# Expert rows of tiles 1 and 2 gathered as joined 8 KB rows, slot by slot, in a fused layer kernel

## The chip, the cores and the metric

One core of one Trainium2 chip runs the whole kernel. The metric is the device time of one execution in microseconds (us). Its median over 3 runs was 1422.61 us (1419.26 to 1423.8).

## What is computed

One layer of a diffusion transformer on 384 tokens (128 context tokens, 256 latent tokens), width 1024, all in f32: modulation, differential attention and a gated DeltaNet side by side, an output projection, and then PEER expert retrieval, which is where the change lies. Cut to that:

```python
def peer(h, w_pq, sub_keys, expert_u, expert_v):     # 8 heads, 2 x 128 keys, top 16
    q = (hf @ w_pq).reshape(T, PEER_HEADS, 2, PEER_DK // 2)
    s = jnp.einsum('thpd,hpnd->thpn', q, sub_keys)
    sv, si = lax.top_k(s, PEER_TOPK)
    cand = ...                                       # 16 x 16 sums per head
    top_s, pos = lax.top_k(cand, PEER_TOPK)
    eidx = ...                                       # 128 experts of 16384 for each token
    gates = jax.nn.softmax(top_s, axis=-1)
    a_sel = hf . expert_u[eidx]
    coef = gates * jax.nn.gelu(a_sel)
    return sum over the 128 experts of coef * expert_v[eidx]
```

Each token takes 128 experts, each a row of 1024 f32 (4 KB) in expert_u and one in expert_v. That is 384 x 128 x 2 rows of 4 KB, 403 MB of gathered data.

## The kernel before, in words

Tokens lie in three tiles (NT = 3) of 128, one token in each partition. A tile has SLOTS = 128 expert slots, and two halves a of HALF = 64 slots. The choice of experts (choice_steps, L473) runs by quarters of 32 slots on VectorE (DVE): `top_key`, `pair_sums`, `top_pair`, `places`, `chosen` twice and `experts`, which writes the indices of the quarter; its scores come from `query` and `key_score` on TensorE (PE).

A **U gather** (`u_rows`, L967, the DMA at L977) is one indirect DMA on GpSimd (POOL): for slot n it brings to each partition its token's row of expert_u, 128 rows, 512 KB. VectorE's `dot` (L2086) multiplies it by the token's h (hnow, in PSUM) and sums it into coef[:, n]. When the 64 dots of a half are done, `coef` (ACT L1305, DVE L2101, PE) applies Gelu, multiplies by the gates and transposes, and `fill` (ACT L1318, L1324) spreads coefficients into W. A **V gather** (`v_rows`, L981, the DMA at L988) brings rows of expert_v by `rowT`, the transposed indices: one gather carries the 64 experts of each of two tokens, and a `v_batch` (PE, L1357) takes four such gathers and multiplies them by 128 x 32 blocks of W into acc, 8 matmuls with 512 columns in four column strips. After the last batch of a tile, `take` (L2112, L2118) multiplies by the gate and adds to xs, `last_norm` (L2124 to L2128) normalizes, and SP stores y (L885). So the gathers run in an order of halves: 64 U, 64 V, 64 U, 64 V of tile 0, then of tile 1, then of tile 2, 768 in all (`gather_order`, HALVES, ALONE).

Rows land in slots of 4 KB per partition. STAGES lists which are usable at which place in the order; from place 208 on there are 13: twelve in the buffer big and one in hT. `row_homes` gives each gather the slot that was used longest ago, and `row_free` (L948) makes POOL wait until the user of that slot's last row has finished (`dot_ready` for U rows, `vsum_done` for V rows).

The order of instructions on PE, DVE, ACT and POOL is made when the kernel is built: each step has costs by engine and a list of the steps it follows (`layer_steps`, `expert_steps`). `Plan.ranked` sorts the steps by the longest chain to the end, plus the head start of the table EARLIER, and `place` puts each in the first gap of its engines that holds it. Each engine runs its list strictly in that order. DVE takes 5.7 for a `top_key`, 1.16 for a `dot`; PE takes 3.6 for half a `query` in this plan.

The weight chunks of `query` of tiles 1 and 2 are shared. Chunk (pq, 2, 1) is loaded by SP (L853) when `query` (0, 2) of tile 2 is done, so the second half of tile 1's choice comes after that, and so does tile 2's.

Of the kernel before, what the change touches and what calls it, by code (L numbers as in the profile page):

```python
# [11 lines left out]
P = 128  # L12
D = 1024
KD = D // P
NT = 3
# [62 lines left out]
HALVES = [(t, a) for t in range(NT) for a in range(2)]  # L78
ALONE = {(0, 0): 64, (0, 1): 64, (1, 0): 64, (1, 1): 64, (2, 0): 64}
# [3 lines left out]
def gather_order():  # L83


    out = [("gu", 0, n) for n in range(HALF)]
    for k, (t, a) in enumerate(HALVES):
        mine = [("gv", t, a, b, j) for b in range(BATCHES) for j in range(QUADS)]
        following = [("gu", u, HALF * c + n) for u, c in HALVES[k + 1:k + 2] for n in range(HALF)]
        first = ALONE.get((t, a), 0)  # L90
        out += mine[:first]
        for n in range(0, len(mine) - first, QUADS):
            out += mine[first + n:first + n + QUADS] + following[n:n + QUADS]
        rest = len(mine) - first
        out += following[rest:]
    return out
# [6 lines left out]
def row_homes():  # L103


    out, uses, last = {}, [0] * (ROWS + 13), [-1] * (ROWS + 13)
    for n, g in enumerate(GATHERS):
        slot = min([homes for until, homes in STAGES if n < until][0], key=lambda s: last[s])
        uses[slot] += 1
        out[g] = (slot, 16 * uses[slot], GATHERS[last[slot]] if last[slot] >= 0 else None)  # L110
        last[slot] = n
    return out
# [11 lines left out]
OPS_ROWS = [g for g in GATHERS if HOMES[g][0] > ROWS + 8]  # L124


def row_user(gather):

    return ("dot",) + gather[1:] if gather[0] == "gu" else ("v_batch",) + gather[1:4]
# [30 lines left out]
EARLIER = {('experts', 0, 0, 0): 200.0, ('slot_gates', 1, 0): 15.0, ('experts', 1, 0, 0): 50.0, ('experts', 1, 0, 1): 50.0, ('dn_done', 1, 1): 50.0, ('v_batch', 0, 0, 15): 100.0, ('dn_done', 2, 1): 100.0, ('dn_done', 1, 0): 100.0, ('dot', 0, 63): 100.0, ('slot_gates', 2, 0): 100.0, ('coef', 1, 0): 200.0, ('qk_turn', 2): 150.0, ('dn_scores', 1, 0): 200.0, ('value', 2, 3): 100.0, ('dn_p', 1, 1, 3): 75.0, ('o_turn', 2): 100.0, ('da_turn', 2): 15.0, ('query', 3, 1): 200.0, ('expert_rows', 0, 0): 150.0, ('dn_scores', 2, 0): 200.0, ('top_key', 0, 0): 50.0, ('mod', 5): 30.0, ('value', 1, 3): 30.0, ('qk_turn', 1): 100.0, ('coef', 0, 1): 100.0, ('experts', 2, 0, 1): 50.0, ('top_key', 2, 0): 100.0, ('token', 1, 2): 200.0, ('resid', 0, 1): 15.0, ('mod', 9): 15.0, ('experts', 0, 0, 1): 15.0, ('experts', 0, 1, 0): 30.0, ('experts', 2, 1, 1): 100.0, ('dn_vb', 2, 0): 15.0, ('dn_vb', 1, 1): 100.0, ('h_turn', 2): 100.0, ('dn_vb', 2, 1): 75.0, ('dn_done', 2, 0): 50.0, ('expert_rows', 0, 1): 15.0}  # L160
# [312 lines left out]
def choice_steps(add, t):  # L473
# [16 lines left out]
    for hh in range(2):  # L490
        for q in range(2):
# [5 lines left out]
            add(("experts", t, hh, q), ("DVE", 0.5), after=[("chosen", t, hh, q, 1), ("expert_rows", t, 0) if hh else None]  # L497
# [3 lines left out]
        add(("expert_rows", t, hh), ("PE", 0, 0.2, ("expert_rows", t, hh), 1), ("DVE", 0.5),  # L501
            after=[("experts", t, hh, 0), ("experts", t, hh, 1), ("dot", 0, SLOTS - 1) if t == 2 else None])


def expert_steps(add):

    for n, g in enumerate(GATHERS):
        t = g[1]
        after = [("@", 1, GATHERS[n - 1])] if n else [(k,) + td for td in PAIRS[0] for k in ("dn_scores", "dn_qg")]
        after += [("experts", t, g[2] // HALF, g[2] // QUARTER % 2)] if g[0] == "gu" else [("expert_rows", t, g[2])]  # L510
        slot, _, back = HOMES[g]
        if back:
            after.append(row_user(back))
# [6 lines left out]
        add(g, ("POOL", 1.12), ("DMA", 0, 1.12, None), ("LATE", 0, 1.2, None), after=after)  # L520
    for k, (t, a) in enumerate(HALVES):
        before = HALVES[k - 1] if k else None
        if t and not a:
            add(("h_load", t), ("ACT", 1.4), after=[("dot", t - 1, SLOTS - 1), ("h_turn", t)])
        for n in range(HALF * a, HALF * a + HALF):
            add(("dot", t, n), ("DVE", 1.16), after=[("gu", t, n), ("dot", t, n - 1) if n else ("h_load", t) if t else ("h_turn", 0)])
        add(("coef", t, a), [("ACT", 0, 3.5), ("DVE", 2.1, 0.4), ("PE", 2.6, 0.15, ("coef", t, a), 1)],
            after=[("dot", t, HALF * a + HALF - 1), ("slot_gates", t, a), ("mod_turn", 11)] + [("dn_decay",) + td for td in PAIRS[2]] + [("fill",) + HALVES[k - 2] + (FILLS - 1,) if k > 1 else None])
        for b in range(BATCHES):
            if b % 4 == 0:  # L530
# [5 lines left out]
                after=[("gv", t, a, b, QUADS - 1), ("fill", t, a, b // 4), ("take", t - 1) if t and not a and not b else None,  # L536
                       ("v_batch", t, a, b - 1) if b else ("v_batch",) + before + (BATCHES - 1,) if k else None])
        if a:
            add(("take", t), ("DVE", 3.0), after=[("v_batch", t, 1, BATCHES - 1), ("gate", 1, min(t, 1), 1),
# [22 lines left out]
def program(nc, counts, x, cst, msk, par, wch, wba, kcT, vc, s0, subk, eu, ev, nout,  # L562
# [4 lines left out]
    with ctx:  # L567
# [134 lines left out]
        def row(slot):  # L702

            if slot == ROWS + 8:
                return hT[:, 0].rearrange("p k n -> p (k n)")
            if slot > ROWS + 8:
# [1533 lines left out]
```

## Time and profile before

| | before |
|---|---|
| median of 3 runs | 1422.61 us (1419.26 to 1423.8) |
| span of the profiled execution | 1577.7 us (its own unprofiled time isn't given) |
| PE, DVE, ACT, POOL busy | 865.6, 813.6, 277.6, 749.9 us |
| DMA, mean over the span | 486.09 MB, 308 GB/s |
| issue of the first and last gather | 276.6 us, 1559.0 us |

The profiled execution is 155 us longer than the median of the runs. In the windows below the columns are the stretch in us from the span's start, its length, the busy time of PE, PEld (weight load), DVE, ACT and POOL with their instruction counts, the mean granted TensorE clock (1.00 is 2.4 GHz, 0.50 is 1.2 GHz), the busy share of the 16 DMA engines, and GB/s. In a timeline a row is: start us, length us, engine, line, operation, out<-in, count, and in brackets the idle time before it and what ended it.

### The profile page before, as it was taken

Reading aid. Unit: us, or ns where it says so; the run is one execution under the profiler, and the core shown is the slowest. Engines: PE = TensorE matmul, PEld = TensorE weight load, DVE = VectorE, ACT = ScalarE, POOL = GpSimd, SP = SyncE. Lnnn points to the kernel's source line nnn. Section 1 sums busy time; section 2 is a strip of 40 time slices with the busy share of each in tenths; the row PEclk is TensorE's granted clock in tenths of the full one; section 3 lists DMA queues with packets and bytes.
Section 4 is the critical chain, followed back from the end, with each engine's and each line's share of the span. In section 5 each row is a group of like instructions: output and inputs, shape, how many; then the busy total and the mean of one; then the engine's idle time right before and its main releaser. Section 6 shows DMA issues by size and latency. Waiting matters only on the chain.

```text
span 1577.7 us, 14365 instructions
## 1 busy us (share of the span) xinstructions
PE 865.6 (55%) x4990; PEld 500.8 (32%) x4990; DVE 813.6 (52%) x2047; ACT 277.6 (18%) x662; POOL 749.9 (48%) x794
## 2 busy tenths in 40 slices
PE   4999998799567776787620675400442005500254
PEld 2566867556353355543210651000110001100010
DVE  2443234687484277851597146897515760087301
ACT  4234443122241232421000020000100000000000
POOL 0001000453446644456676226676667666676663
PEclk9998999899798999899755887655685557755576
DMA  9234446995659988799999729999999999999996
GB/s 394 91 140 151 161 167 254 375 390 215 240 182 356 343 310 316 241 395 352 364 404 357 297 72 375 359 397 364 354 376 376 402 346 335 359 402 364 347 368 234
DMA packets 120295, 486.09 MB, mean 308 GB/s; under 512 B 13344, under 2 KB 14240, under 8 KB 115616
## 3 DMA queue, kind: packets, MB, share of 16 engines
q0 software_dynamic: 111056, 404.28, 68.4%
q1 hardware_dynamic: 9168, 80.90, 13.2%
q8 instruction: 41, 0.67, 0.2%
q14 instruction: 30, 0.25, 0.0%
HBM read 482.50 MB, written 2.62 MB: 307 GB/s over the span
## 4 chain that ended last, share of the span: by engine, by line
DVE 17%; issue 17%; PE 14%; POOL 13%; DMA 6%; another core or an unknown queue 4%; ACT 1%; POOLq 0%; DVEq 0%; ACTq 0%
PE bank L1357 13%; DVE big L2086 11%; POOL big L988 10%; DMA big<-in_ev,idx 2%; POOL big L977 2%; DMA big<-in_ev,rowT 2%; DMA big<-in_eu,consts 2%; DVE hT L2086 1%; POOL hT L988 1%; PE bank L1363 1%; PE bank L1475 0%; DVE big L1876 0%; DVE dn_tok L1970 0%; DVE sq L2112 0%
## 5 line engine op out<-in xcount | busy, mean ns | idle before, releaser
L2086 DVE CUSTOM_DVE_ANT_0 big<-big,hnow 128x1024 f32<-128x1024 f32 x315 | 377.4, 1218 | 193.2 <-DMA big<-in_eu,consts 127.9
L1357 PE MATMUL bank<-big,W 128*32 128x512 f32 x1296 | 259.7, 835 | 167.6 <-DMA big<-in_ev,idx 64.0
L977 POOL DMA_INDIRECT big<-in_eu,consts x236 | 223.4, 947 | 103.4 <-issue 71.6
L988 POOL DMA_INDIRECT big<-in_ev,rowT x197 | 190.5, 967 | 153.5 <-PE bank L1357 76.6
L1357 PE MATMUL bank<-hT,wring 128*128 128x128 f32 (+1 forms) x896 | 143.3, 319 | 40.4 <-issue 32.2
L1363 PE MATMUL bank<-consts 128*128 128x128 f32 x6 | 2.4, 392 | 294.3 <-DVE consts L2101 294.3
L1357 PEld LDWEIGHTS bank<-big,W 128*32 128x32 f32 x1296 | 53.4, 136 | 332.3 <-issue 319.7
L988 POOL DMA_INDIRECT big<-in_ev,idx x118 | 111.7, 947 | 68.2 <-issue 33.3
L1357 PEld LDWEIGHTS bank<-hT,wring 128*128 128x128 f32 x896 | 120.4, 202 | 64.6 <-issue 41.4
L1357 PE MATMUL bank<-big 128*128 128x128 f32 x720 | 100.1, 288 | 40.6 <-issue 23.0
L977 POOL DMA_INDIRECT big<-in_eu,idx x79 | 75.1, 951 | 99.1 <-DVE coef L2086 57.4
L1357 PEld LDWEIGHTS bank<-big 128*128 128x128 f32 x720 | 91.1, 200 | 48.8 <-issue 28.7
L1363 PEld LDWEIGHTS bank<-consts 128*128 128x128 f32 x6 | 1.0, 161 | 298.4 <-DVE consts L2101 298.2
L1357 PE MATMUL bank<-hT,W 128*32 128x512 f32 x120 | 83.9, 839 | 10.3 <-DMA big<-in_ev,rowT 5.9
L1357 PE MATMUL bank<-wring,hT 128*128 128x512 f32 x176 | 78.8, 606 | 6.1 <-DMA wring<-in_wch 6.1
L1003 ACT ACTIVATE big<-bank 128x512 f32<-128x512 f32 x84 | 49.6, 597 | 110.8 <-PE bank L1357 84.9
L1876 DVE TENSOR_TENSOR big<-bank,masks 128x512 f32<-128x512 f32 x42 | 28.8, 688 | 73.9 <-PE bank L1475 54.6
L900 POOL DMA_DIRECT2D out_o_ck<-tok x1 | 0.7, 732 | 138.4 <-ACT tok L1003 138.4
L1357 PE MATMUL bank<-wring,W 128*32 128x512 f32 x300 | 50.9, 670 | 12.5 <-DMA wring<-in_wch 6.5
L988 POOL DMA_INDIRECT wring<-in_ev,rowT x39 | 37.0, 949 | 40.1 <-DVE coef L2086 14.5
L1305 ACT ACTIVATE coef<-coef 128x64 f32<-128x64 f32 x4 | 1.0, 256 | 285.6 <-remote 139.7
L2112 DVE TENSOR_TENSOR sq<-bank,gate 128x512 f32<-128x512 f32 x6 | 4.1, 688 | 88.8 <-PE bank L1357 88.0
(294 smaller groups left out, 1379.8 us busy)
## 6 DMA issues: line engine op xcount, KB each, us to landing
wring<-in_wch SPq DMA_DIRECT2D x29, 2048.0 KB, 9.2
big<-in_wch SPq DMA_DIRECT2D x6, 1536.0 KB, 8.8
big<-in_eu,consts POOLq DMA_INDIRECT x236
big<-in_ev,rowT POOLq DMA_INDIRECT x197
tok<-in_wch SPq DMA_DIRECT2D x6, 512.0 KB, 9.9
big<-in_ev,idx POOLq DMA_INDIRECT x118
xs<-in_x SPq DMA_DIRECT2D x1, 1536.0 KB, 6.6
out_y<-xs SPq DMA_DIRECT2D x3, 512.0 KB
```

Source lines behind the costliest of these rows:

```text
L900: pool.dma_start(o_ck, tok[:, 0, 512:1024]).then_inc(cache_out, 16)
L977: nc.gpsimd.indirect_dma_start(row(slot), None, eu, bass.IndirectOffsetOnAxis(ap=idx[t][:, n:n + 1], axis=0)).then_inc(rows_in[slot], 16)
L988: nc.gpsimd.indirect_dma_start(row(slot), None, ev, bass.IndirectOffsetOnAxis(ap=rowT[t][:, n:n + 1], axis=0)).then_inc(rows_in[slot], 16)
L1003: nc.scalar.activation(out, ps(*job)[:, 0:n] if src is None else src, func, **kw).then_inc(*reads(sig, key, *job))
L1305: nc.scalar.activation(c, c, ACT.Gelu).then_inc(*gelu_ready.next(t, a))
L1357: return nc.tensor.matmul(out, lhsT, rhs, start=first, stop=last)
L1363: ins = nc.tensor.transpose(b[:, i * P:(i + 1) * P], src[:, i * P:(i + 1) * P], ident)
L1876: V.tensor_tensor(heads(PM[pi][d]), heads(ps(*job)[:, :]), rep(level_mask(d, lv), 4), ALU.mult).then_inc(*reads(p_ready, (t, d, lv), *job))
L2086: V.tensor_tensor_reduce(row(slot), row(slot), hnow[:, :], 1.0, 0.0, ALU.mult, ALU.add, coef[t % 2][:, n:n + 1]).then_inc(dot_ready, 1)
L2112: ins = V.tensor_tensor(sq[:, :], acc[h][:, :], gate[:, v, s], ALU.mult)
```

## The change

Tile 0 stays as it is: U and V gathers of 4 KB rows, 64 by 64, in the same slots. For tiles 1 and 2 a new input `euv` holds each expert's U row and V row side by side (8 KB). One gather per slot (`wide_rows`, 128 rows, 1 MB) brings both by the slot's own index. So 512 gathers of 512 KB become 256 of 1 MB. `dot` reads the first 4 KB. After each pair of dots, ACT applies Gelu to the pair's two coefficients, DVE's new `spread` writes for each slot a 128 x 128 diagonal matrix (identity times coefficient times gate), and PE's new `v_slot` multiplies it by the last 4 KB of the row into acc, two matmuls with 512 columns for each slot. The transposes, the coef step, the fills and `rowT` go for tiles 1 and 2. Wide slots are pairs of the 4 KB slots: six in big for tile 1 (each waits for the last users of both rows under it), ten for tile 2 (four more in wring, after the last `query`). Eight diagonal matrices fit in W (SPREADS), and `v_slot` (1, 0) waits for tile 0's `take`.

```diff
-HALVES = [(t, a) for t in range(NT) for a in range(2)]
-ALONE = {(0, 0): 64, (0, 1): 64, (1, 0): 64, (1, 1): 64, (2, 0): 64}
+HALVES = [(0, 0), (0, 1)]
+WIDE0 = ROWS + 13
+WIDE = {1: range(WIDE0, WIDE0 + 6), 2: range(WIDE0, WIDE0 + 10)}
+SPREADS = 8
...
+    for a in range(2):
+        out += [("gu", 0, HALF * a + n) for n in range(HALF)]
+        out += [("gv", 0, a, b, j) for b in range(BATCHES) for j in range(QUADS)]
+    return out + [("gw", t, n) for t in (1, 2) for n in range(SLOTS)]
...
-EARLIER = {... ('experts', 2, 1, 1): 100.0, ...}
+EARLIER = {... ('experts', 2, 1, 1): 400.0, ... ('experts', 2, 1, 0): 400.0, ('last_norm', 0): 300.0, ('last_norm', 1): 150.0}
...
+        add(g, ("POOL", 1.12), ("DMA", 0, 2.5 if g[0] == "gw" else 1.12, None), ("LATE", 0, 1.2, None), after=after)
...
+            add(("gelu", t, b), ("ACT", 0.3), after=[("dot", t, 2 * b + 1)])
+            add(("spread", t, b), ("DVE", 0.45),
+                after=[("gelu", t, b), ("slot_gates", t, 2 * b // HALF),
+                       ("v_slot", 1 + old // SLOTS, old % SLOTS) if old >= 0 else ("v_batch", 0, 1, BATCHES - 1)])
+            for n in (2 * b, 2 * b + 1):
+                add(("v_slot", t, n), ("PE", 1.75),
+                    after=[("spread", t, b), ("v_slot", t, n - 1) if n else ("take", t - 1)])
...
+            def wide_rows(t, n):
+                if n % QUARTER == 0:
+                    pool.wait_ge(*idx_ready.at(t, n // QUARTER))
+                slot, _ = row_slot(("gw", t, n))
+                row_free(("gw", t, n))
+                nc.gpsimd.indirect_dma_start(row(slot), None, euv,
+                                             bass.IndirectOffsetOnAxis(ap=idx[t][:, n:n + 1], axis=0)
+                                             ).then_inc(rows_in[slot], 16)
...
+            def gelu(t, b):
+                c = coef[t % 2][:, 2 * b:2 * b + 2]
+                act.wait_ge(dot_ready, SLOTS * t + 2 * b + 2)
+                nc.scalar.activation(c, c, ACT.Gelu).then_inc(*gelu_ready.next(t, b))
...
+            def v_slot(t, n):
+                if n == 0:
+                    pe.wait_ge(*acc_read.at(t - 1))
+                slot, count = row_slot(("gw", t, n))
+                pe.wait_ge(rows_in[slot], count)
+                pe.wait_ge(*spread_ready.at(t, n // 2))
+                for h in range(2):
+                    ins = mm(acc[h][:, :], spread_at(t, n), row(slot)[:, D + 512 * h:D + 512 * h + 512], n == 0, n == SLOTS - 1)
+                ins.then_inc(vsum_done, 1)
...
+            def spread(t, b):
+                old = SLOTS * (t - 1) + 2 * b + 1 - SPREADS
+                dve.wait_ge(vsum_done, 2 * BATCHES + max(old + 1, 0))
+                dve.wait_ge(*gelu_ready.at(t, b))
+                for n in (2 * b, 2 * b + 1):
+                    ins = V.scalar_tensor_tensor(out=spread_at(t, n), in0=ident, scalar=coef[t % 2][:, n:n + 1],
+                                                 in1=gates[t][:, n:n + 1].to_broadcast([P, P]), op0=ALU.mult, op1=ALU.mult)
+                ins.then_inc(*spread_ready.next(t, b))
...
+        "euv": np.concatenate([a["expert_u"][0], a["expert_v"][0]], 1), "nout": rows(a["norm_out"]),
```

## Rows read from the trace of the kernel before

**Rows 1.** The page: span, busy times, and the slices of 39.4 us.

```profile
span 1577.7 us, 14365 instructions
...
PE 865.6 (55%) x4990; PEld 500.8 (32%) x4990; DVE 813.6 (52%) x2047; ACT 277.6 (18%) x662; POOL 749.9 (48%) x794
...
PEclk9998999899798999899755887655685557755576
DMA  9234446995659988799999729999999999999996
```

**Rows 2.** Windows: all of tiles 1 and 2, then single stretches.

```profile
774.00:1560.00 786.00, 252.47 (x1479) 96.17 (x1479) 410.59 (x975) 36.03 (x92) 487.34 (x512) 0.63 0.92 351
...
881.00:935.00 54.00, 46.16 (x385) 42.45 (x387) 5.67 (x23) 11.21 (x22) 0.51 (x1) 0.94 0.32 128
935.00:1008.00 73.00, 39.16 (x213) 8.19 (x205) 52.40 (x268) 3.58 (x11) 50.22 (x51) 0.73 0.95 349
...
1096.00:1189.00 93.00, 41.73 (x226) 9.14 (x226) 36.64 (x136) 9.09 (x23) 61.25 (x65) 0.68 0.97 364
1189.00:1277.00 88.00, 5.49 (x32) 1.18 (x32) 67.55 (x111) 0.00 (x0) 60.39 (x65) 0.54 0.98 381
...
1410.00:1440.00 30.00, 0.00 (x0) 0.00 (x0) 24.84 (x41) 0.00 (x0) 22.27 (x24) 0.50 1.03 409
```

**Rows 3.** The page's DMA queues: packets, MB, share of 16 engines.

```profile
q0 software_dynamic: 111056, 404.28, 68.4%
q1 hardware_dynamic: 9168, 80.90, 13.2%
```

**Rows 4.** The chain of waits from 774 us: start, length, what.

```profile
811.20 2.42 issue
...
828.00 51.60 issue
```

**Rows 5.** The page's costliest groups: dots and U gathers of tiles 1, 2.

```profile
L2086 DVE CUSTOM_DVE_ANT_0 big<-big,hnow 128x1024 f32<-128x1024 f32 x315 | 377.4, 1218 | 193.2 <-DMA big<-in_eu,consts 127.9
...
L977 POOL DMA_INDIRECT big<-in_eu,consts x236 | 223.4, 947 | 103.4 <-issue 71.6
```

**Rows 6.** Timeline: one v_batch at either clock, with the last gather.

```profile
1155.75 1.92 PE L1357 MATMUL bank<-big,W 128*32 128x512 f32 x16 [2.06 <-DMA big<-in_ev,rowT]
...
1559.04 0.95 POOL L988 DMA_INDIRECT big<-in_ev,idx  x1 [0.30 <-issue]
1564.94 3.64 PE L1357 MATMUL bank<-big,W 128*32 128x512 f32 x16 [6.99 <-DMA big<-in_ev,idx]
```

**Rows 7.** Timeline: Gelu's table load, the half's product, two small DVE operations.

```profile
927.47 1.28 ACT L1305 ACT_TABLE_LOAD   x1
928.76 0.26 ACT L1305 ACTIVATE consts<-consts 128x64 f32<-128x64 f32 x1
929.12 0.29 DVE L2101 TENSOR_TENSOR consts<-consts,params 128x128 f32<-128x128 f32 x1 [54.41 <-ACT consts L1305]
...
714.10 0.23 DVE L2052 SCALAR_TENSOR_TENSOR E<-E 128x64 f32<-128x64 f32 x1
```

**Rows 8.** Timeline: a gather after a pause of POOL, and its dot.

```profile
1198.66 0.95 POOL L977 DMA_INDIRECT big<-in_eu,consts  x1 [3.21 <-remote]
...
1203.01 1.22 DVE L2086 CUSTOM_DVE_ANT_0 big<-big,hnow 128x1024 f32<-128x1024 f32 x1 [0.79 <-DMA big<-in_eu,consts]
```

**Rows 9.** Windows, DVE alone: the choice of one quarter, twice.

```profile
932.10:947.10 15.00, 14.21 (x73) 0.73 0.62 199
...
748.40:766.00 17.60, 14.16 (x72) 0.82 0.98 361
```

**Rows 10.** Timeline of SP and PE: a weight chunk's load and a query.

```profile
889.24 0.33 SPq L853 DMA_DIRECT2D wring<-in_wch  x1
...
899.45 7.31 PE L1357 MATMUL bank<-hT,wring 128*128 128x128 f32 x64
```

**Rows 11.** Window with PE busy 72% of the time.

```profile
550.00:600.00 50.00, 35.85 (x247) 28.82 (x236) 36.21 (x76) 18.75 (x51) 20.77 (x22) 0.93 0.88 315
```

More of the change, by code:

```diff
@@ L103, in row_homes @@
 def row_homes():
-    out, uses, last = {}, [0] * (ROWS + 13), [-1] * (ROWS + 13)
+    out, uses, last = {}, [0] * (WIDE0 + 10), [-1] * (WIDE0 + 10)
     for n, g in enumerate(GATHERS):
-        slot = min([homes for until, homes in STAGES if n < until][0], key=lambda s: last[s])
+        homes = WIDE[g[1]] if g[0] == "gw" else [homes for until, homes in STAGES if n < until][0]
+        slot = min(homes, key=lambda s: last[s])
         uses[slot] += 1
-        out[g] = (slot, 16 * uses[slot], GATHERS[last[slot]] if last[slot] >= 0 else None)
+        under = [slot]
+        if last[slot] < 0 and WIDE0 <= slot < WIDE0 + 6:
+            under = [2 * (slot - WIDE0), 2 * (slot - WIDE0) + 1]
+        out[g] = (slot, 16 * uses[slot], [GATHERS[last[u]] for u in under if last[u] >= 0])
         last[slot] = n
@@ L121, in row_slot @@
     return HOMES[gather][:2]
-OPS_ROWS = [g for g in GATHERS if HOMES[g][0] > ROWS + 8]
+OPS_ROWS = [g for g in GATHERS if HOMES[g][0] in range(ROWS + 9, WIDE0)]
 def row_user(gather):
-    return ("dot",) + gather[1:] if gather[0] == "gu" else ("v_batch",) + gather[1:4]
+    return {"gu": ("dot",) + gather[1:], "gv": ("v_batch",) + gather[1:4], "gw": ("v_slot",) + gather[1:]}[gather[0]]
 class Counts:
@@ L496, in choice_steps @@
                 add(("chosen", t, hh, q, w), ("DVE", 2.0), after=[("places", t, hh, q), ("chosen", t, hh, q, 0) if w else None])
-            add(("experts", t, hh, q), ("DVE", 0.5), after=[("chosen", t, hh, q, 1), ("expert_rows", t, 0) if hh else None]
+            add(("experts", t, hh, q), ("DVE", 0.5), after=[("chosen", t, hh, q, 1), ("expert_rows", 0, 0) if hh and not t else None]
                 + [("dn_decay", u, d) for u in (1, 2) for d in range(2) if t])
@@ L519, in expert_steps @@
             after.append(("dn_done",) + PAIRS[2][slot // 4])
-        add(g, ("POOL", 1.12), ("DMA", 0, 1.12, None), ("LATE", 0, 1.2, None), after=after)
-    for k, (t, a) in enumerate(HALVES):
[L522 to L526, printed above, removed]
+        add(g, ("POOL", 1.12), ("DMA", 0, 2.5 if g[0] == "gw" else 1.12, None), ("LATE", 0, 1.2, None), after=after)
+    for t in range(NT):
+        if t:
+            add(("h_load", t), ("ACT", 1.4), after=[("dot", t - 1, SLOTS - 1), ("h_turn", t)])
+        for n in range(SLOTS):
+            add(("dot", t, n), ("DVE", 1.16), after=[("gw" if t else "gu", t, n), ("dot", t, n - 1) if n else ("h_load", t) if t else ("h_turn", 0)])
+    for k, (t, a) in enumerate(HALVES):
         add(("coef", t, a), [("ACT", 0, 3.5), ("DVE", 2.1, 0.4), ("PE", 2.6, 0.15, ("coef", t, a), 1)],
-            after=[("dot", t, HALF * a + HALF - 1), ("slot_gates", t, a), ("mod_turn", 11)] + [("dn_decay",) + td for td in PAIRS[2]] + [("fill",) + HALVES[k - 2] + (FILLS - 1,) if k > 1 else None])
+            after=[("dot", t, HALF * a + HALF - 1), ("slot_gates", t, a), ("mod_turn", 11)] + [("dn_decay",) + td for td in PAIRS[2]])
         for b in range(BATCHES):
@@ L1654, in v_batch @@
             def v_batch(t, a, b):
-                if (a, b) == (0, 0) and t:
-                    pe.wait_ge(*acc_read.at(t - 1))
                 if b % 4 == 0:
```

98 lines of the change are left out of this document (54 added, 44 removed).

## The prediction, made before the changed kernel was run

> **What bounds the kernel now.** I read the page first: no engine is busy for more than 55% of the span, but from the fifteenth slice on the DMA row shows mostly nines [rows 1]. So I cut the stretch of tiles 1 and 2 into its halves with windows. There DMA is busy 0.92 of 786 us [rows 2]. In the middle of a run of U gathers it moves 409 GB/s, so 524.3 KB take 1.28 us; that is the best pace, and 512 gathers at it are 656 us. POOL needs 0.95 us for a gather [rows 5] and in such a run 22.27 / 24 = 0.93 us busy of every 1.25 us: it is close behind. PE and DVE take turns: in a V half PE is busy 42 us of 93, in a U half 5 of 88, while DVE is busy 68 of 88 in a U half [rows 2].
>
> One hole stands out: 881 to 935 us, DMA busy 0.32. The chain of waits shows why: a `query` of tile 2 crawls, one wait of 2.4 us after the other, and then 51.6 us of "issue", a wait for nothing the profile shows [rows 4]; the loads and choices behind it come late. The profiled execution is 155 us over the median of the runs. I take this hole (54 us) as part of the excess and spread the other 101 us over the 768 gathers, 0.13 us each. That gives for an execution without the profiler: 740 us up to tile 1's first gather (774 less 34), 665 us for tiles 1 and 2 (786 less 54 less 67), 17.7 us after them: 1422.7, against the median 1422.6. The split is an assumption. Its other end is that the excess lies before 774 us as far as it can, and that the stretch of tiles 1 and 2 keeps some of its losses in V halves (93 us where 82 would do): then it is some 690 us long. I sum against 1422.6, which stands 155 us under the profiled span.
>
> **The change, part by part.**
>
> Bytes stay: 256 gathers of 1 MB for 512 of 512 KB. The queue of gathers spends 0.684 x 1577.7 x 16 / 404.28 = 42.7 us of engine time on a MB, that of the weights, whose rows are longer (8.8 KB a packet on average), 41.2 [rows 3]. Rows of 8 KB lie between no gain and this ratio of 0.965. I take 2.48 us for a gather, nearly all of the gain, since the second queue's rows are the nearest in size: 256 x (2.56 - 2.48) = **21 us less** (ends 0 and 24).
>
> POOL issues half as many gathers: 0.95 us, or at worst twice that, beside 2.48 us of DMA. No cost either way.
>
> The dots stay, 1.14 us apart when nothing holds them (1.22 busy [rows 5]). A spread is two operations of 128 x 128; its nearest rows are 0.23 us for 64 columns and 0.29 us for 128 [rows 7], so 0.5 us a pair (0.4 to 0.6). DVE then needs 1.14 + 0.25 = 1.39 us of each 2.48 us: hidden while nothing else is on DVE. Gelu, 0.26 us or less, follows every second dot on ACT, with a table load of 1.28 us when another function came between [rows 7]. ACT is nearly idle here [rows 2].
>
> PE: a v_batch is 8 matmuls of 512 columns in four strips; it takes 1.92 us at the upper clock level and 3.64 us at the lower one [rows 6], that is, the time of two full-width matmuls one after the other. A v_slot has just two. So PE works 1.75 to 1.9 us in 2.48 us at 2.4 GHz, instead of for four gathers in 5.1 us. Hidden at the upper level. At 1.2 GHz a v_slot takes 3.5 us, over the gather's 2.48. Which level it is, the windows tell for two loads: 0.68 on average in V halves with PE busy 45% [rows 2], 0.93 where it is busy 72% [rows 11]; a v_slot each 2.48 us is 70 to 75%, so I take the upper level and no cost. By the lower one the sum would be 256 x 1.0 = 260 us longer. [...]
>
> Entry: `v_slot` (1, 0) waits for tile 0's take, and the first wide slot for its last batches but one. About 6 us of gathers are in flight at that point [rows 6], so I charge **3 us** (0 to 8). Tail: before, one v_batch follows the last landing; now a dot, Gelu, a spread and two v_slots: 1.2 + 0.3 + 0.5 + 3.6 against 1.9 or 3.6, **3 us more** (2 to 6).
>
> What is gone with the alternation is DVE's rest. At 774 us tile 1 has its first half's indices; two quarters of tile 1 and four of tile 2 are still to be chosen, 14.2 us of DVE each [rows 9], 85 us, and the queries for them, 7.3 us each on PE [rows 10], six of them, 44 us. Now this lies mostly in tile 1's V halves, where DVE has no dots (935 to 1008 us [rows 2]) and 13 slots buffer what is in flight. Behind the change tile 1 has a dot every 2.48 us, without a break, and six wide slots. **The ring's slack.** A slot comes round every 6 x 2.48 = 14.9 us. Around it: issue to landing with a short queue 4.3 us for 512 KB [rows 8] and 1.3 us for the second half of the row, 2.5 us for its partner, 1.2 us dot, 0.3 us Gelu, 0.5 us spread, 1.8 us v_slot, 0.3 us of hops: 12.2 us. So 2.7 us of slack at the upper clock level, 1 us at the lower. A `top_key`, which the plan takes at 5.7 us, doesn't fit between two slots, nor does half a query of 3.6 us; and the plan holds a gather landed 2.65 us after its issue, so it sees more slack than there is. DVE has 2.48 - 1.39 = 1.09 us free in a slot. With one step of about 2 us of choice between two slots, a quarter is spread over eight slots, 14.2 us of work into 8.7 us of room: 5.5 us late. Six quarters: 33 us, of which the slack and tile 2's ten slots save some. I take **28 us** (0 if the choice is done by single small steps or before 774 us; 80 if each quarter is run as one block). POOL's next gather waits for the slot, so each such delay is DMA idle time and is never made up.
>
> Sum: 1422.6 - 21 + 3 + 3 + 28 = **1436 us**.
>
> The weights' two chunks after 774 us (the second at [rows 10]) are loaded in both kernels and cost the same.
>
> **The rivals.**
>
> *The ring holds (faster), 0.36.* The order made by the plan places the choice in small steps, or early: DVE's total in tile 1 is 128 x 1.39 + 85 = 263 us of 317, so there is room. For it: a quarter consists of seven steps, most near 2 us, which is under the slack. It decides if each delay stays under 2.7 us. Then the loss is 0 to 10 us, and the losses of V halves go too (up to 25 us by the other split): 1422.6 - 21 + 6 + 5 = 1413, and down to 1390.
>
> *Gain and loss cancel, 0.12.* Loss near 15 us: 1418 to 1427.
>
> *The clock takes PE over the gathers (slower), 0.04.* If PE never left the lower level: 1422.6 - 21 + 6 + 260 = 1668 us. Against it speak the row at 72% and that a PE which falls behind works without a break. A few spells of it are in the range. [...]
>
> *The change doesn't do what it says*: if 8 KB rows are moved as two of 4 KB each, the 21 us go, and the forecast becomes 1457. Inside the range.
>
> **How the numbers follow.** The forecast (choice work stalls the six-slot ring, loss of 20 to 80 us) has 0.48: its own range is 1427 to 1480. With the rivals: low end 1393 (ring holds, losses of V halves gone), high end 1474 (loss near 66 us); blocks as a whole and the clock are left out. Under 1418.3 is faster and over 1426.9 slower, 0.3% being about what a measurement of this kernel can tell from no change. Faster 0.37, same 0.11, slower 0.52.
>
> **What would show it.** Right: in tile 1 the DMA row falls under 0.9, POOL's gathers wait for PE's v_slots by more than the 2.48 us of DMA, and the holes coincide with top_key and query steps; in tile 2 gathers follow each other at 2.5 us, DMA near 1.0; PE's granted clock over 0.85. Wrong: tile 1 as dense as tile 2 (the ring holds); gathers 2.56 us apart or more (no gain from long rows); v_slots of 3.5 us with PE busy all the time (the clock). It would also be wrong if tile 1's first wide gather came much later than tile 1's first gather now, at 774 us in the profile.

## The result: 1472.8 us, 3.6% slower, and where the 50 us are

The changed kernel took 1472.8 us (median of 4 runs, 1467.92 to 1475.68) against 1422.4 us (4 runs, 1419.26 to 1423.8) for the kernel before: a ratio of 1.036, 95% interval 1.0325 to 1.0391. The forecast was 1436 us. The direction was right, the loss was more than three times the size. The profile of the changed kernel is of its fastest run (1467.9 us), so the two spans below differ by 43.4 us and not by 50.

The page of the changed kernel, with the lines that answer to [rows 1]:

```profile
span 1466.0 us, 14643 instructions
...
PE 1127.3 (77%) x4982; PEld 638.9 (44%) x4982; DVE 890.2 (61%) x2291; ACT 293.2 (20%) x733; POOL 506.1 (35%) x538
...
PEclk9999999988998999989987999989999999999999
DMA  9326345889368998988399999998999999999995
```

PE works 262 us more than in [rows 1], at a clock that hardly leaves 2.4 GHz, and POOL 244 us less. From the twenty-first slice on DMA shows nines but for one 8 and the end; the loss isn't there. The slice with a 3 just ahead of it (the twentieth, 696 to 733 us) lies in tile 0, which the change was to leave as it was.

To say what moved, I need a profile of before without the 155 us of excess. A second profile of the same, unchanged kernel gives it (the first experiment below). Its span is 1422.6 us. These are the issues of the first gather of tile 1, the first of tile 2 and the last one, from POOL's timeline, and the last landing from the chain of waits. First the kernel before, second profile:

```profile
728.41 0.95 POOL L977 DMA_INDIRECT big<-in_eu,consts  x1 [0.31 <-issue]
...
1072.10 0.95 POOL L977 DMA_INDIRECT big<-in_eu,consts  x1 [0.30 <-issue]
...
1401.18 8.94 DMA big<-in_ev,idx
```

The same in the changed kernel:

```profile
788.11 0.94 POOL L1030 DMA_INDIRECT big<-in_euv,consts  x1 [5.31 <-PE bank L1405]
...
1120.74 0.94 POOL L1030 DMA_INDIRECT wring<-in_euv,consts  x1 [0.30 <-issue]
...
1431.35 19.45 DMA big<-in_euv,consts
```

| us | before | after | difference |
|---|---|---|---|
| up to tile 1's first gather | 728.4 | 788.1 | +59.7 |
| tile 1, first gather to tile 2's first | 343.7 | 332.6 | -11.1 |
| tile 2, first gather to last landing (1410.1, 1450.8) | 338.0 | 330.1 | -7.9 |
| after the last landing | 12.5 | 15.2 | +2.7 |
| span | 1422.6 | 1466.0 | +43.4 |

So tiles 1 and 2, which the change rewrote, became 19 us shorter, and tile 0 became 60 us longer.

**What happens in tile 0.** Windows of 20 us over its last V half (columns as in [rows 2]), before (second profile) and after:

```profile
680.00:700.00 20.00, 12.99 (x80) 5.16 (x77) 0.00 (x0) 1.29 (x4) 15.12 (x17) 0.74 1.03 411
700.00:720.00 20.00, 12.94 (x102) 5.08 (x104) 14.49 (x74) 2.51 (x5) 15.43 (x16) 0.91 1.03 409
```

```profile
680.00:700.00 20.00, 20.00 (x180) 19.94 (x179) 14.49 (x74) 5.17 (x9) 0.00 (x0) 1.00 0.50 178
700.00:720.00 20.00, 19.21 (x172) 19.04 (x172) 19.00 (x105) 2.54 (x5) 0.00 (x0) 1.00 0.34 132
```

Before, POOL issues 16 or 17 gathers in 20 us and DMA is full. After, POOL issues none at all and PE is busy for the whole time. PE's timeline of the changed kernel says with what, and POOL's timeline what it cost:

```profile
661.86 3.64 PE L1405 MATMUL bank<-big,W 128*32 128x512 f32 x16 [3.94 <-DMA big<-in_ev,rowT]
...
667.19 14.61 PE L1405 MATMUL bank<-hT,wring 128*128 128x128 f32 x128
...
683.50 14.46 PE L1405 MATMUL bank<-hT,wring 128*128 128x128 f32 x128
...
699.72 7.31 PE L1405 MATMUL bank<-hT,wring 128*128 128x128 f32 x64
...
708.79 14.46 PE L1405 MATMUL bank<-hT,wring 128*128 128x128 f32 x128
...
725.40 1.01 POOL L1020 DMA_INDIRECT big<-in_ev,rowT  x1 [49.93 <-PE bank L1405]
```

A query is 64 of these matmuls (hT times the weights in wring, [rows 10]). After the second V batch (661.86) PE runs 128 + 128 + 64 + 128 = 448 of them, seven queries, before it turns to the third. By then all thirteen row slots hold V rows that wait for PE, and POOL stands for 49.9 us. Grouped by engine and line, with these queries and DVE's MAX8 over 80 candidates (four for a quarter's choice) counted in stretches: in the kernel before, second profile, from 600 to 728.4 us and in tile 1

```profile
L1357 PE MATMUL bank<-hT,wring 128*128 128x128 f32 x128 | 15.2, 278 | 0.2 <-issue 0.2
L1967 DVE MAX8 E<-xo 128x8 f32<-128x80 f32 x8 | 1.6, 236 | 0.1
...
L1357 PE MATMUL bank<-hT,wring 128*128 128x128 f32 x384 | 46.0, 283 | 3.2 <-issue 3.2
L1967 DVE MAX8 dn_tok<-ops 128x8 f32<-128x80 f32 x16 | 3.1, 234 | 0.2
L1967 DVE MAX8 E<-ops 128x8 f32<-128x80 f32 x8 | 1.6, 236 | 0.1
```

and in the changed one from 600 to 788.1 us and in tile 1:

```profile
L1405 PE MATMUL bank<-hT,wring 128*128 128x128 f32 x512 | 58.1, 275 | 0.0
L2024 DVE MAX8 dn_tok<-ops 128x8 f32<-128x80 f32 x12 | 2.3, 235 | 0.2
L2024 DVE MAX8 E<-xo 128x8 f32<-128x80 f32 x8 | 1.5, 235 | 0.1
L2024 DVE MAX8 E<-ops 128x8 f32<-128x80 f32 x4 | 0.8, 235 | 0.1
...
L2024 DVE MAX8 E<-ops 128x8 f32<-128x80 f32 x4 | 0.8, 234 | 0.0
L2024 DVE MAX8 dn_tok<-ops 128x8 f32<-128x80 f32 x4 | 0.8, 234 | 0.0
```

Before, six of the eight queries and six of the eight quarters of tiles 1 and 2 are worked on in tile 1. The six queries run from 737.5 to 793.7 us, beside U gathers, which wait for DVE alone (the first V gather of tile 1 is issued at 815.4 us), and most of the choice runs behind that, beside V gathers. DMA keeps 408 GB/s over tile 1 all the same. After, all eight queries and six quarters come ahead of tile 1, and only two quarters lie in it.

### The profile page after: what moved, and what is told of

It is laid out like the page before. It is cut to its first block, busy times and chain, and to the rows that moved or that the text cites. A ratio compares the mean times of both kernels' runs of the same rounds, so it can differ in the third digit from the quotient of the medians.

```text
span 1466.0 us, 14643 instructions
## 1 busy us (share of the span) xinstructions
PE 1127.3 (77%) x4982; PEld 638.9 (44%) x4982; DVE 890.2 (61%) x2291; ACT 293.2 (20%) x733; POOL 506.1 (35%) x538
## 4 chain that ended last, share of the span: by engine, by line
DMA 29%; PE 20%; DVE 9%; POOL 6%; issue 4%; ACT 1%; DVEq 0%; POOLq 0%; ACTq 0%
DMA big<-in_euv,consts 27%; PE bank L1405 19%; DVE big L2142 4%; POOL big L1020 3%; POOL wring L1020 2%; DVE W L2166 2%; DMA big<-in_ev,rowT 1%; DMA wring<-in_eu,idx 1%; PE bank L1411 0%; PE bank L1523 0%; DMA big<-in_eu,idx 0%; DVE wring L2142 0%; POOL hT L1020 0%; DVE big L1933 0%; DVE xs L2184 0%
## 5 line engine op out<-in xcount | busy, mean ns | idle before, releaser
L1405 PE MATMUL bank<-big,W 128*128 128x512 f32 (+1 forms) x1164 | 445.2, 643 | 172.8 <-DVE W L2166 146.3
L1405 PEld LDWEIGHTS bank<-big,W 128*128 128x128 f32 (+1 forms) x1164 | 163.9, 172 | 432.4 <-issue 430.7
L1030 POOL DMA_INDIRECT big<-in_euv,consts x204 | 194.6, 954 | 322.6 <-PE bank L1405 318.0
L1405 PE MATMUL bank<-wring,W 128*32 128x512 f32 (+1 forms) x508 | 149.6, 657 | 57.7 <-DVE W L2166 36.0
L2142 DVE CUSTOM_DVE_ANT_0 wring<-wring,hnow 128x1024 f32<-128x1024 f32 x77 | 92.9, 1219 | 36.5 <-DMA wring<-in_euv,consts 34.9
L1405 PE MATMUL bank<-big 128*128 128x128 f32 x720 | 97.1, 282 | 18.6 <-DVE big L1933 12.2
L1405 PEld LDWEIGHTS bank<-wring,W 128*32 128x32 f32 (+1 forms) x508 | 50.3, 151 | 136.4 <-issue 130.9
L1020 POOL DMA_INDIRECT big<-in_ev,rowT x78 | 75.7, 971 | 85.0 <-PE bank L1405 62.0
L1030 POOL DMA_INDIRECT wring<-in_euv,consts x52 | 49.1, 944 | 83.3 <-PE bank L1405 79.8
L2166 DVE SCALAR_TENSOR_TENSOR W<-consts,coef,params 128x128 f32<-128x128 f32 x128 | 39.5, 349 | 22.1 <-ACT coef L1357 22.1
L2166 DVE SCALAR_TENSOR_TENSOR W<-consts,params 128x128 f32<-128x128 f32 x128 | 39.5, 350 | 20.5 <-ACT consts L1357 20.3
```

What stands on the lines that cost most here:

```text
L1020: nc.gpsimd.indirect_dma_start(row(slot), None, ev, bass.IndirectOffsetOnAxis(ap=rowT[t][:, n:n + 1], axis=0)).then_inc(rows_in[slot], 16)
L1030: nc.gpsimd.indirect_dma_start(row(slot), None, euv, bass.IndirectOffsetOnAxis(ap=idx[t][:, n:n + 1], axis=0)).then_inc(rows_in[slot], 16)
L1405: return nc.tensor.matmul(out, lhsT, rhs, start=first, stop=last)
L2142: V.tensor_tensor_reduce(u, u, hnow[:, :], 1.0, 0.0, ALU.mult, ALU.add, coef[t % 2][:, n:n + 1]).then_inc(dot_ready, 1)
L2166: ins = V.scalar_tensor_tensor(out=spread_at(t, n), in0=ident, scalar=coef[t % 2][:, n:n + 1], in1=gates[t][:, n:n + 1].to_broadcast([P, P ...
```

## The experiments

**The kernel before once more.** No edit.

> The kernel before, profiled a second time. If the hole of 54 us in tile 1's first V half (881 to 935 us in the first profile), with the query whose matmuls crawl ahead of it, is the kernel's own, it comes again at the same place with the same length, give or take 5 us. If it is a product of the profiler, the crawl is elsewhere or of another length (by over 15 us), since the profiled execution was 155 us over the unprofiled ones.

Measured: 1424.5 us, span 1422.6 us. There is no crawl and no hole: tile 1 has 408 GB/s from end to end. The hole of [rows 4] and the other 101 us were a product of that one profiled execution.

```profile
728.00:1072.00 344.00, 144.92 (x948) 71.03 (x950) 250.44 (x708) 25.06 (x58) 246.46 (x257) 0.71 1.02 408
1072.00:1410.00 338.00, 91.81 (x538) 20.16 (x530) 163.35 (x267) 10.94 (x34) 243.56 (x256) 0.66 1.01 404
```

**Only the order of the queries, in the kernel before.**

```diff
-EARLIER = {... ('query', 3, 1): 200.0, ...}
+EARLIER = {... ('query', 3, 1): 700.0, ... ('query', 3, 2): 500.0}
```

> The kernel before with one thing of the change alone: PE's order puts seven of the eight queries of tiles 1 and 2 ahead of the third V batch of tile 0's second half, as the changed kernel has them. Nothing else differs: 4 KB rows, alternation of U and V, 13 slots in all. Theory A (the loss is made before tile 1: queries put ahead of V batches that hold the slots): 35 to 50 us slower than before, 1457 to 1475 us, though some of it is given back, since the V halves of tile 1 lose their queries. Rival (the kernel before pays the same queries in tile 1's V halves anyway, and the loss of the changed kernel comes from its six-slot ring): 1415 to 1430 us.

Measured: 1473.7 us (1467.78 to 1480.08), ratio 1.036 [1.0308, 1.0412], the same as the whole change. POOL stands with nine V gathers issued, before the first V batch, and tile 1 starts at 788.7 us. The order isn't quite that of the changed kernel: PE runs six queries ahead of the first V batch (384 matmuls, 667.1 to 717.0 us), where the changed kernel runs seven behind the second.

```profile
719.17 0.95 POOL L988 DMA_INDIRECT big<-in_ev,rowT  x1 [58.57 <-PE bank L1357]
```

No wide row, no spread, no `v_slot` is needed for the loss: theory A holds and its rival falls. Tile 1 gets only 12 us back (331.9 for 343.7 us).

**The V batches first, in the changed kernel.**

```diff
-EARLIER = {...}
+EARLIER = {... ('gw', 1, 0): 200.0}
```

> The changed kernel with its order corrected by hand: the first wide gather (and with it the V batches of tile 0 that free its slot) ranks 200 us earlier, so that the V batches come ahead of most queries. Theory A alone: the hole before tile 1 goes (tile 1's first gather near 740 us unprofiled) and nothing comes in its place: about 1425 us. Theory B (the choice work has no cover beside a six-slot ring): tile 1 begins some 45 us earlier but takes 60 to 90 us longer, as queries and key choices now run beside its ring; the time is 1475 to 1510 us.

Measured: 1500.1 us (1494.86 to 1507.16), ratio 1.053 [1.0482, 1.0578]. Tile 1's first gather is issued at 730.2 us, as in the kernel before, but tile 1 now takes 427.9 us, 95 us longer. Of the 95 us, 80 are lost at the start: after four gathers POOL stands for 65.8 us and, two gathers later, for 23.3, so that the seventh is issued 96.0 us behind the first, in the changed kernel 16.4 (timelines of POOL and of PE).

```profile
733.97 0.94 POOL L1030 DMA_INDIRECT big<-in_euv,consts  x1 [0.30 <-issue]
800.70 0.95 POOL L1030 DMA_INDIRECT big<-in_euv,consts  x1 [65.79 <-issue]
...
826.20 0.94 POOL L1030 DMA_INDIRECT big<-in_euv,consts  x1 [23.31 <-PE bank L1405]
```

```profile
729.22 14.83 PE L1405 MATMUL bank<-hT,wring 128*128 128x128 f32 x128
...
787.94 7.31 PE L1405 MATMUL bank<-hT,wring 128*128 128x128 f32 x64
...
797.11 0.62 PE L1405 MATMUL bank<-big,W 128*32 128x512 f32 x2
...
822.58 11.93 PE L1405 MATMUL bank<-big,W 128*128 128x512 f32 x24 [23.55 <-DVE W L2166]
```

The head start reached all V batches but the last. The first wide gather doesn't wait for that one, so in the plan's ranks it stays at 503, below seven queries (628 to 556). PE runs the seven in one block between the last batch but one and the last (729 to 795 us). The fifth wide slot lies over rows of the last batch, and the first `v_slot` waits for `take`, which follows that batch and 21 us of choice on DVE (797.9 to 818.9 us). So the time is the one that theory B gave, with 95 us where it had 60 to 90, but most of the loss is made at the entry into the ring and not beside a running ring. The other 15 us fall behind the entry, where three quarters of the choice lie beside the ring and in the changed kernel two. What queries in small steps cost beside a running ring, this run doesn't show. Together with the runs before: a block of queries ahead of V batches costs 60 us in the V half of tile 0 and, with the choice behind it, 80 us at the entry into the wide slots, and the six beside U gathers cost nothing that shows in DMA's 408 GB/s.

**The old table of head starts, in the changed kernel.**

```diff
-EARLIER = {... ('experts', 2, 1, 1): 400.0, ... ('experts', 2, 1, 0): 400.0, ('last_norm', 0): 300.0, ('last_norm', 1): 150.0}
+EARLIER = {... ('experts', 2, 1, 1): 100.0, ...}
```

> The changed kernel with the table of early steps of the kernel before (no 400 us for the choices of tile 2's second half, none for the last norms). By both theories, A and B, the hole before tile 1 shrinks by some 15 us, and the queries that left it come back beside tile 1's ring: 1465 to 1480 us. If only the place before tile 1 matters, and not what runs in tile 1: 1455 to 1460 us.

Measured: 1467.3 us (1466.34 to 1471.66), ratio 1.032 [1.0282, 1.0359]. Tile 1 starts 11 us earlier, at 777.1 us, and takes 7.5 us longer (340.1). Of the 60 us the table makes 11; the rest comes from the plan itself. Given the intervals, the time alone doesn't separate this kernel from the changed one; the two starts do. Here tile 1 (777.1 to 1117.2 us) has two queries and no quarter of the choice; the last two quarters lie in tile 2. The first row is from the stretch of tile 1, the second from that of tile 2:

```profile
L1405 PE MATMUL bank<-hT,wring 128*128 128x128 f32 x128 | 14.9, 276 | 0.0
...
L2024 DVE MAX8 dn_tok<-ops 128x8 f32<-128x80 f32 x8 | 1.5, 234 | 0.1
```

So tile 1 on six slots is no shorter without the choice beside it.

**Only tile 2 wide.** Tiles 0 and 1 keep rows of 4 KB, halves, `coef`, `fill` and `rowT` as before; `wide_rows`, `gelu`, `spread` and `v_slot` serve tile 2 alone.

```diff
-HALVES = [(0, 0), (0, 1)]
-WIDE = {1: range(WIDE0, WIDE0 + 6), 2: range(WIDE0, WIDE0 + 10)}
+HALVES = [(t, a) for t in range(2) for a in range(2)]
+WIDE = {2: range(WIDE0, WIDE0 + 10)}
...
-EARLIER = {... the table of after ...}
+EARLIER = {... the table of before ..., ('gw', 2, 0): 163.0}
... (the steps and waits of tile 1 as in the kernel before)
```

> Tiles 0 and 1 as before (4 KB rows, alternation of U and V halves, thirteen slots, the order of work the same up to tile 2, with 163 us put onto the rank of tile 2's first wide gather for the 128 gathers that its chain has lost), and only tile 2, beside which no choice work is left, gathers joined 8 KB rows into ten slots. Theory A and B together (what the change loses is the choice work's cover, before tile 1 or beside its ring; what it gains is the pace of 8 KB rows, 7.8 us in one tile, less 2.7 us of longer tail): tile 1's first gather at 728 us in the profile as before, 5 us faster than before in all, 1415 to 1420 us. Rival (joined rows cost something of their own, at the entry into the wide slots or in the spreads and v_slots beside the end): 1424 us or more.

Measured: 1421.8 us (12 runs, 1418.81 to 1428.87), ratio 0.9981 [0.9958, 1.0005]. Tile 1 starts at 727.3 us and the 50 us are gone, but of the 5 us hoped for only half came, and the interval still touches no change. The rival names the place: the entry into the wide slots.

```profile
1082.45 0.94 POOL L1030 DMA_INDIRECT big<-in_euv,consts  x1 [10.64 <-PE bank L1405]
```

The first wide slot lies over two row slots whose V rows had just been requested; POOL waits 10.6 us for them to land and be summed.

**The same, with the wide slots in wring first.**

```diff
-WIDE = {2: range(WIDE0, WIDE0 + 10)}
+WIDE = {2: [*range(WIDE0 + 6, WIDE0 + 10), *range(WIDE0, WIDE0 + 6)]}
```

> As the kernel in which only tile 2 gathers joined rows, but tile 2 begins with the four wide slots that lie in the ring of the weights, which have been free since the last query, and only then takes the six that lie over tile 1's row slots. In the run before, tile 2's first gather was issued 10 us later than in the kernel before (1082.4 against 1072.1 us), and the pace behind it was 2.49 us a gather. If that delay is the wait for both row slots under a wide slot, it goes: 8 to 12 us less than that kernel, 1409 to 1415 us, faster than both. Rival (the delay lies in the V batches or in tile 1 itself): within 3 us of it, 1419 to 1425 us.

Measured: 1415.0 us (12 runs, 1412.57 to 1420.2), ratio 0.9951 [0.9931, 0.9971]: 7 us faster than before and the fastest of all kernels here. Against the kernel with the other order of slots it is 6.8 us, not the 8 to 12 expected, and 2 of these lie ahead of tile 1 (its first gather is issued at 725.3 us, there at 727.3). Four 1 MB gathers (10 us of DMA) go out before the wait:

```profile
1070.29 0.95 POOL L1030 DMA_INDIRECT wring<-in_euv,consts  x1 [0.30 <-issue]
...
1074.04 0.94 POOL L1030 DMA_INDIRECT wring<-in_euv,consts  x1 [0.30 <-issue]
1082.40 0.94 POOL L1030 DMA_INDIRECT big<-in_euv,consts  x1 [7.42 <-PE bank L1405]
```

**Six or ten slots.** Three runs with one number changed each: tile 2 on six slots (twice, since the first set was scattered), and tile 1 on ten.

```diff
-WIDE = {1: range(WIDE0, WIDE0 + 6), 2: range(WIDE0, WIDE0 + 10)}
+WIDE = {1: range(WIDE0, WIDE0 + 6), 2: range(WIDE0, WIDE0 + 6)}
```

> The changed kernel, but tile 2 uses six wide slots like tile 1, with no choice work beside them. My prediction gave a six-slot ring 2.7 us of slack when nothing else runs: then tile 2 keeps its 2.43 us from gather to gather and the time is that of the changed kernel, 1468 to 1476 us. Rival (six slots are too few even without the choice, and tile 1's 2.60 us a gather are the ring's own): tile 2 goes to 2.55 us or more a gather, 15 us or more longer, 1485 us or more.

Measured: 1484.5 us (three runs, 1480.48 to 1490.87; the profiled execution took 1503.38 and is left out), ratio 1.0416 [1.0369, 1.0464]. In that profiled execution tile 1, the same code as in the changed kernel, was 15 us longer, so its profile decides nothing.

> The kernel with six wide slots in tile 2 once more, for a profile at its usual time: the first profile of it took 1503 us where its other runs took 1480 to 1491, and tile 1, which is the same as in the changed kernel, was 15 us longer there too. If six slots cost tile 2 some 10 us by short stalls that ten slots absorb, tile 1 is near the 333 us of the changed kernel and tile 2 takes 338 to 345 us from its first gather's issue to the last landing, against 330. If six slots are too few for the pace itself, the usual gap from gather to gather in tile 2 is over 2.49 us also away from the stalls.

Measured: 1478.9 us (1474.06 to 1488.91), ratio 1.0395 [1.0338, 1.0452]. From tile 1's first gather (788.0 us) to the last landing (1462.5 us) it is 674.5 us against the changed kernel's 662.7, 12 us more. Only a part of them can be tile 2's: from tile 1's first gather to its last, the same code in both, it is 336.1 against 331.4 us, and from tile 2's first gather (1127.8 us) to the last landing 334.7 against 330.1, under the 338 to 345 expected. The intervals of both sets overlap the changed kernel's, so what the four slots are worth to tile 2 stays unclear.

```diff
-WIDE = {1: range(WIDE0, WIDE0 + 6), 2: range(WIDE0, WIDE0 + 10)}
+WIDE = {1: range(WIDE0, WIDE0 + 10), 2: range(WIDE0, WIDE0 + 10)}
```

> The changed kernel, but tile 1 too uses ten wide slots: its last four lie in the ring of the weights and are first used when the last query is done. Tile 2 on six slots cost 15 us unprofiled and went from 2.49 to 2.59 us a gather. If tile 1's 2.60 us a gather are in the same way the six slots' own, tile 1 becomes 10 to 15 us shorter, 1457 to 1463 us. Rival (tile 1's loss comes from the key choices and gates that run beside it on DVE): within 4 us of the changed kernel.

Measured: 1458.7 us (1452.11 to 1462.72), ratio 1.0245 [1.0199, 1.0291], its interval clear of the changed kernel's. Tile 1 starts at 792.2 us, so the hole before it is still there; first gather to last landing takes 650.0 us, 13 less. That is what the six-slot ring cost tile 1. The expectation of 10 to 15 us holds, and its rival, that the loss is the choice's whatever the slots, falls. How such a ring loses it, the time from issue to landing of tile 1's gathers shows: the changed kernel first, then ten slots.

```profile
DMA to landing us min/median/max: 5.5/8.4/12.7
```

```profile
DMA to landing us min/median/max: 6.1/17.8/20.0
```

Ten slots keep a median of 17.8 us from issue to landing, six only 8.4, and the pace is 418 against 401 GB/s. What stands above the 5.5 us of the shortest one is queue, and as long as there is a queue a stall of DVE or PE leaves DMA busy. By these medians the reserve is an estimated 3 us with six slots (8.4 - 5.5) and 12 with ten (17.8 - 5.5). The number of slots is a reserve of time; the best pace is DMA's. One of the stalls in tile 1's ring (timeline of DVE and ACT, changed kernel):

```profile
954.66 0.19 DVE L2076 TENSOR_TENSOR E<-E 128x32 f32<-128x32 f32 x1
954.88 0.23 ACT L1341 ACTIVATE E<-E 128x32 f32<-128x32 f32 x1 [4.74 <-DVE E L2076]
955.13 1.28 ACT L1357 ACT_TABLE_LOAD   x1
...
956.76 0.61 DVE L2166 SCALAR_TENSOR_TENSOR W<-consts,params 128x128 f32<-128x128 f32 x2 [0.52 <-ACT consts L1357]
957.53 4.08 PE L1405 MATMUL bank<-big,W 128*128 128x512 f32 x5 [4.15 <-DVE W L2166]
```

`places` (twelve small operations) stands ahead of the spread, its exponential (L1341) costs Gelu a table load of 1.28 us, and PE idles for 4.15 us. Behind this and the step of choice at 970 to 991 us stand two of the four waits of POOL over 5 us inside tile 1 (6.8 us at 961 and 9.6 at 992; the others, 9.2 us at 804 and 5.1 at 819, follow the entry).

**The pace of the two row lengths by itself.** To the changed kernel, behind its last output row block, gathers are added that nothing reads: 128 of joined rows into six slots,

```diff
+            base = [max(c for s, c, _ in HOMES.values() if s == WIDE0 + i) for i in range(6)]
+            pool.wait_ge(*y_ready.at(2))
+            for i in range(128):
+                s = i % 6
+                if i >= 6:
+                    pool.wait_ge(rows_in[WIDE0 + s], base[s] + 16 * (i // 6))
+                nc.gpsimd.indirect_dma_start(big[:, 2 * D * s:2 * D * (s + 1)], None, euv,
+                                             bass.IndirectOffsetOnAxis(ap=idx[2][:, i:i + 1], axis=0)
+                                             ).then_inc(rows_in[WIDE0 + s], 16)
... (a wait for the last of them)
```

> The changed kernel with extra work behind its end: when the last output row block is ready, 128 more gathers of joined 8 KB rows (134 MB, the indices of tile 2) into six slots, which wait for nothing but their own landing. It is there for the pace alone. If the row's length is what sets the pace: 2.49 us a gather, 421 GB/s, some 320 us more than the changed kernel, about 1793 us.

or 256 of 4 KB rows (eu and ev in turn) into twelve.

> The same with 256 gathers of 4 KB rows of U and V in turn (the same 134 MB, the same indices) into twelve slots. If the row's length sets the pace: 1.28 us a gather, 409 GB/s, some 328 us more than the changed kernel, 8 us over the run with 8 KB rows. If 4 KB rows lost time only through the halves' turns in the kernel before: as fast as the 8 KB rows, within 2 us. If POOL's 0.95 us a gather and the gap behind it bound them: more than 1.30 us a gather, 15 us or more over the run with 8 KB rows.

Measured: 1796.6 us (1790.25 to 1803.34, ratio 1.2585 [1.2532, 1.2638]) and 1809.1 us (1806.42 to 1818.02, ratio 1.2704 [1.2647, 1.2761]); 12.5 us between them, where the expectation had 8 and the rival with POOL 15 or more. Windows of the same 250 us in both, 8 KB rows first:

```profile
1520.00:1770.00 250.00, 0.00 (x0) 0.00 (x0) 0.00 (x0) 0.00 (x0) 95.08 (x101) 0.50 1.01 422
```

```profile
1520.00:1770.00 250.00, 0.00 (x0) 0.00 (x0) 0.00 (x0) 0.00 (x0) 188.31 (x201) 0.50 1.03 409
```

With nothing else running 8 KB rows move at 422 GB/s and 4 KB rows at 409, as in the tiles. POOL doesn't bound the short ones, though it comes close: it issues one every 1.25 us (0.94 and a gap of 0.30), and DMA takes 1.28 for each. So issue to landing grows from 5.1 to 15.1 us over the run, until the twelve slots are full at 1764 us and the last 18 gathers wait for a landing, 1.28 us apart. The row's length sets the pace: at these rates 134.2 MB take 318 or 328 us, 10 us apart, so 20 us for two tiles.

## Why the prediction was right or wrong

- **The profile of before, right.** I took the hole of 54 us as the profiler's and put tile 1's first gather at 740 us; the clean profile has 728.4, no hole, and 681.7 us for tiles 1 and 2, between my 665 and the 690 of the other end. The split did not carry the miss. What I read from it on tile 1 was wrong in one place: I put queries and choice "mostly in tile 1's V halves", and in the clean profile all six queries lie in its first U half.
- **21 us of longer rows, right.** 20 us by the windows above; from the first to the last issue of tile 2, 329.1 / 127.5 = 2.58 us for two gathers before and 310.6 / 127 = 2.45 us for one after, the latter with the deeper queue of ten slots. The Trainium skill, page "DMA: Bandwidth & Descriptors", section "Anatomy of one DMA — SWDGE (gpsimd) path", gives each DMA about 2.0 us of fixed time beside the time for its bytes. An estimate that charged this in full for 256 DMAs less would be 512 us; the trace has 20, since here several gathers are in flight at once.
- **No cost on PE through the clock, right.** The granted clock is 0.96 in tile 1 and 0.98 in tile 2, where PE is busy 71% and 75%; before it was 0.71 and 0.66 at 42% and 27%. These windows of the changed kernel also give the pace, 401 and 421 GB/s:

```profile
794.00:1121.00 327.00, 231.98 (x489) 91.37 (x490) 218.22 (x498) 20.96 (x71) 117.88 (x125) 0.96 0.98 401
1121.00:1432.00 311.00, 231.91 (x504) 92.05 (x502) 195.55 (x383) 17.58 (x69) 120.81 (x128) 0.98 1.01 421
```

  PE's pauses between two pairs of v_slots are 1.3 us long, and behind them a pair's eight matmuls take 3.67 us, 0.46 each:

```profile
949.71 3.67 PE L1405 MATMUL bank<-big,W 128*128 128x512 f32 x8 [1.27 <-DVE W L2166]
```

  Behind the pause of 4.15 us (the row at 957.53 above) five matmuls take 4.08 us, 0.82 each, the lower level. The Trainium skill, page "TensorE: Matmul & The Clock Gate", section "HAM oscillation — how this bites in real kernels", describes a kernel whose clock falls back at every DMA wait of 3 to 5 us between short bursts. The trace agrees: the long pause brings the fall, the short ones don't.
- **Small costs.** A spread pair takes 0.61 us from start to end (the row at 956.76) where I had 0.5; still hidden. The tail is 2.7 us longer, where I had 3. The entry waits 5.3 us (the row at 788.11) where I had 3; into tile 2 it is 10.6 us when no wring slot is taken first.
- **The ring's slack of 2.7 us, right; what it costs, wrong.** I had 12.2 us of round trip in the 14.9 us in which six slots come round, with 5.6 us to the landing. The shortest landing is 5.5 us, and by the medians the reserve is 8.4 - 5.5 = 2.9 us. But the term of 28 us was for six quarters and six queries beside tile 1's ring. Two quarters and no query lie there, and the ring costs 13 us by the run with ten slots. Nor are these 13 us shown to be the choice's: two waits of POOL stand behind it, and the run with the V batches first loses 15 us more with three quarters there; but in the run with the old table tile 1 has no quarter beside it and takes 340.1 us against 332.6. How they divide among the choice, last_norm, the gates and the ring's own round trip stays open. The sign that I had set for being right, DMA under 0.9 in tile 1, didn't come: it is 0.98.
- **The step that failed: "At 774 us tile 1 has its first half's indices; two quarters of tile 1 and four of tile 2 are still to be chosen".** I kept the place of the queries and the choice fixed and asked only what they would meet there. But the order is made anew by the plan for the changed kernel, and the plan moved six queries and four quarters (6 x 7.3 us of PE, 4 x 14.2 us of DVE [rows 9, 10]) to before tile 1. A step's rank is the longest chain behind it, and in that chain a gather counts with POOL's 1.12, not with the 2.5 of DMA that the change wrote beside it. With 256 gathers fewer, the V batches of tile 0's second half, which head that chain, fell from 959 to 877 (first to last) to 579 to 503 in the plan's own ranks. Before, one of the eight queries stood above all of them (962) and one among them (918); tile 2's had 729 to 264. After, the eight stand at 633 to 556, those of tile 2's second half lifted by the new 400s in EARLIER, and none can be overtaken by more than a few V batches. The price, for which the forecast had nothing, is 60 us, and the run that only moves queries in the kernel before pays it in full. Most of it comes from the changed ranks and not from the new numbers in EARLIER: with the old table 49 of the 60 us stay.
- **What I charged as "cost the same", wrong.** The two weight chunks of 2 MB went to before tile 1 with their queries (issues at 682 and 698 us for 745 and 754). At 409 GB/s they are an estimated 10 us, which is most of why tile 1 became 11 us shorter in spite of its ring. In the run that only moves queries they go there too (682.8 and 698.9 us), and its tile 1, with 4 KB rows, is 12 us shorter.
- **Slips that changed little.** The upper end of the gain from long rows is 23 us (2.56 x 0.035 x 256), not 24. The forecast's own range ends at 1480, but a loss of 80 us gives 1488. And the plan holds a joined gather landed 4.0 us behind POOL's part of it (2.5, 1.2 and two hops of 0.15), not 2.65.

So the sum, by the profiles: 1422.6 + 60 (the hole) - 20 (row length) - 10 (chunks moved out of tile 1) + 13 (six-slot ring) + 3 (tail) = 1468.6, against a span of 1466.0; 2.6 us are left over. That it closes so well is in part luck: tile 1 of the same code took 332.6, 336.1 and 338.7 us in the profiles of the changed kernel and of the two with gathers behind its end. The forecast had the second and the last term, and 28 for the first and the fourth together. The rival in which the ring holds was nearer to the truth inside the tiles, and still the kernel was slower: none of my cases held a loss in tile 0, and only the last sentence on what would prove me wrong named it. That 1472.8 us still lies under the range's upper end of 1474 is luck: that end stood for 66 us lost beside the ring.

What the profiles don't settle is what a plan with both kept would give: queries that leave the V batches alone and tile 1 wide as well. The one table entry that was tried moved them behind all V batches but the last and made 1500 us. A head start for the last V batch as well wasn't tried, nor other places for the queries.

## What to carry to other kernels

Where the order of instructions is made by a planner, a change of the steps' number or cost changes the order everywhere; compute or at least bound the new order before costing the changed part, and look first at what ranks above what where slots are held. Work that has no slot of its own (here queries and choices) needs a stretch in which the transfers lean on another engine; a layout in which every transfer needs every engine takes that cover away (for queries this is argued from the waits: no run here has more than two of them beside a running ring of such transfers), and the cure was to make the change only where nothing is left to hide. And when a buffer changes its shape, enter it through the parts that are already free.

## What the runs showed of the hardware that was not expected

- A profiled execution can be 155 us (11%) longer than the kernel's median, with a hole of its own, and the next profile of the same kernel has neither (1577.7 and 1422.6 us). One profile's excess isn't spread evenly, and one more profile is cheap.
- The time from issue to landing of a 1 MB gather tells how many are queued more than how long the transfer takes. It is 8.4 us (median) in tile 1 with six slots whose rows wait for three engines, 14.7 with six slots that are asked for again as soon as they land (the run with 8 KB rows behind the end), and 17.8 with ten; the shortest is 5.5.
- PE's granted clock holds near 2.4 GHz (0.98) with a pause of 1.3 us behind every 3.67 us of work, and one pause of 4.15 us was enough for the lower level.
- Eight-KB rows move 3% faster than 4 KB rows, 422 for 409 GB/s, with POOL at 0.94 us for either. With the short rows POOL's 1.25 us a gather is only 2% under DMA's 1.28.
